# Scaling attention probabilities by products with diagonals on TensorE instead of on GpSimd

## What is computed

```python
def masked_softmax(s, mask):
    s = jnp.where(mask, s.astype(jnp.float32), -jnp.inf)
    m = jnp.max(s, axis=-1, keepdims=True)
    m = jnp.where(jnp.isfinite(m), m, 0.0)
    p = jnp.exp(s - m)
    return p / jnp.maximum(jnp.sum(p, axis=-1, keepdims=True), 1e-30)

s = jnp.einsum('bqhd,bkhd->bhqk', qb, k) * scale
p = masked_softmax(s, pos[None, :] <= t[:, None])
o = jnp.einsum('bhqk,bkhd->bqhd', p.astype(dt), v)
```

## Time and profile before

| | us |
|---|---|
| median of 3 runs | 3665.45 |
| fastest, slowest | 3661.15, 3670.55 |
| the profiled execution | 3661.0 |
| its span | 3659.0 |
| TensorE busy in the span | 3529.5 |

### The profile page before, as it was taken

How to read it: one execution, slowest core, us unless ns; L and a number is a source line. 1 busy time by engine, 2 the same in 40 slices (tenths; PEclk the granted TensorE clock), 3 DMA queues, 4 the chain that set the end, 5 groups by cost and what they waited for, 6 DMA issues and landing times. The chain is left out here.

```text
span 3659.0 us, 46860 instructions
## 1 busy us (share of the span) xinstructions
PE 3529.5 (96%) x16596; PEld 2872.5 (79%) x16596; DVE 2066.9 (56%) x3132; ACT 1399.7 (38%) x2450; POOL 1681.2 (46%) x949
## 2 busy tenths in 40 slices
PE   7999999999999999999999999999999999999998
PEld 5877877788878768778888778778877877778876
DVE  5767646212267767462123676558964665658943
ACT  3244652323233436433322446333333446333332
POOL 3337544444434465444443554434543654435543
PEclk9999999999999999999999999999999999999999
DMA  4310023222232100232243220533343220532322
GB/s 151 109 58 30 28 77 115 86 97 92 98 116 94 52 29 24 89 113 92 92 150 127 76 77 23 184 121 109 126 144 117 70 81 33 177 119 103 132 92 86
DMA packets 96595, 346.73 MB, mean 95 GB/s; under 512 B 12464, under 2 KB 13104, under 8 KB 95792
## 3 DMA queue, kind: packets, MB, share of 16 engines
q1 hardware_dynamic: 96432, 344.61, 27.3%
HBM read 338.14 MB, written 6.29 MB: 94 GB/s over the span
## 5 line engine op out<-in xcount | busy, mean ns | idle before, releaser
L226 POOL TENSOR_TENSOR weights_lo<-arena,weights_hi 128x1024 fp32r<-128x1024 f32 x467 | 1174.9, 2516 | 1516.7 <-ACT weights_hi L200 1515.7
L200 ACT ACTIVATE weights_hi<-arena 128x1024 fp32r<-128x1024 f32 x491 | 517.4, 1054 | 624.8 <-PE ps L608 389.8
L294 PE MATMUL ps<-moving_hi,weights_hi 128*128 128x512 f32 x2448 | 639.0, 400 | 21.7 <-ACT moving_hi L242 9.2
L294 PE MATMUL ps<-moving_hi,weights_lo 128*128 128x512 f32 x2448 | 613.8, 393 | 0.0
L294 PE MATMUL ps<-moving_lo,weights_hi 128*128 128x512 f32 x2448 | 606.0, 389 | 0.3 <-DVE moving_lo L269 0.2
L294 PEld LDWEIGHTS ps<-moving_hi,weights_hi 128*128 128x128 f32 x2448 | 461.2, 189 | 144.3 <-ACT moving_hi L242 13.2
L294 PEld LDWEIGHTS ps<-moving_hi,weights_lo 128*128 128x128 f32 x2448 | 466.4, 191 | 97.6 <-POOL weights_lo L226 0.4
L294 PEld LDWEIGHTS ps<-moving_lo,weights_hi 128*128 128x128 f32 x2448 | 458.4, 188 | 96.3 <-DVE moving_lo L269 0.9
L1043 POOL TENSOR_SCALAR arena<-arena 128x128 f32<-128x128 f32 (+2 forms) x240 | 225.1, 950 | 214.3 <-DVE arena L948 133.4
L247 DVE TENSOR_TENSOR moving_lo<-arena,moving_hi 128x512 fp32r<-128x512 f32 x196 | 177.3, 955 | 233.0 <-ACT moving_hi L242 233.0
L999 ACT ACTIVATE arena<-ps,arena 128x512 f32<-128x512 f32 (+1 forms) x320 | 164.8, 525 | 127.4 <-DVE arena L937 126.5
(11 more groups left out here) (354 smaller groups left out, 5279.4 us busy)
## 6 DMA issues: line engine op xcount, KB each, us to landing
arena<-wstream SPq DMA_DIRECT2D x532, 512.0 KB, 3.3
arena<-modw SPq DMA_DIRECT2D x64, 512.0 KB, 3.6
arena<-modw_first SPq DMA_DIRECT2D x32, 512.0 KB, 4.3
layer_input<-arena SPq DMA_DIRECT2D x2, 2048.0 KB, 6.9
arena<-layer_input SPq DMA_DIRECT2D x2, 2048.0 KB, 8.0
arena<-xT SPq DMA_DIRECT2D x1, 2048.0 KB, 8.7
outT<-arena SPq DMA_DIRECT2D x1, 2048.0 KB, 7.0
arena<-con SPq DMA_DIRECT2D x1, 1411.5 KB, 11.1
```

Source lines behind the costliest of these rows:

```text
L200: m.nc.scalar.activation(m.w_hi[:, j % 2, :], slab(m, base + at), ACT.Copy).then_inc(hi_ready, 1)
L226: m.nc.gpsimd.tensor_tensor(m.w_lo[:, j % 2, :], slab(m, base + (j if at is None else at)), m.w_hi[:, j % 2, :].bitcast(F32), ALU.subtract)\
L294: mm = m.nc.tensor.matmul(bank, unit_tile(w, k), a[:, k, :], start=(p == 0 and k == 0), stop=(p == 2 and k == KD - 1))
```

## The change

VectorE makes four diagonals per unit, one for each query block, in two buffers of four (the tile `spread` is twice as large, which `m.two_tiles` gives). TensorE multiplies all ten blocks by the diagonal of their query block. GpSimd scales nothing, and the semaphore `scaled` is gone. GpSimd still waits for `inverted` before the half of low weights that belongs to a unit.

```diff
-        def diagonal(u):
-            return spread[:, (u % 2) * P:(u % 2 + 1) * P]
+        def diagonal(u, qt):
+            return spread[:, (u % 2 * TT + qt) * P:(u % 2 * TT + qt + 1) * P]
...
             def turn(u):
-                pe.wait_ge(scaled, u + 1)
-                pe.wait_ge(diag_done, u + 1)
+                pe.wait_ge(diag_done, TT * u + TT)
...
-                            if qt < TT - 1:
-                                mm = nc.tensor.transpose(o, block, m.ident)
-                            else:
-                                mm = nc.tensor.matmul(o, block, diagonal(u), start=True, stop=True)
+                            mm = nc.tensor.matmul(o, block, diagonal(u, qt), start=True, stop=True)
...
                 dve.wait_ge(exped, 3 * u + 3)
-                if u >= 2:
-                    dve.wait_ge(scaled, u - 1)
...
-                nc.vector.tensor_scalar(diagonal(u), m.ident, rinv[:, s + 3:s + 4], None, ALU.mult).then_inc(diag_done, 1)
+                for qt in range(TT):
+                    nc.vector.tensor_scalar(diagonal(u, qt), m.ident, rinv[:, s + qt:s + qt + 1], None, ALU.mult).then_inc(diag_done, 1)
...
             for u in range(NU):
-                j, b = divmod(u, nb)
-                s = 4 * (u % 2)
-                pool.wait_ge(inverted, (u + 1) * (1 if weights(j, b) is None else 2))
-                for qt in range(TT - 1):
-                    v = prob[:, u % 2, PROB_AT[qt]:PROB_AT[qt] + P * (qt + 1)]
-                    r = nc.gpsimd.tensor_scalar(v, v, rinv[:, s + qt:s + qt + 1], None, ALU.mult)
-                r.then_inc(scaled, 1)
+                pool.wait_ge(inverted, (u + 1) * (1 if weights(*divmod(u, nb)) is None else 2))
```

More of the change, by code:

```diff
@@ L838, in attention_stage @@
     mx, sums, rinv = m.small[:, 0:8], m.small[:, 8:16], m.small[:, 16:24]
-    with stage(m, "scores maxed exped inverted scaled transposed hi_out lo_out pv_done side_out half_out o_out diag_done tapped "
+    with stage(m, "scores maxed exped inverted transposed hi_out lo_out pv_done side_out half_out o_out diag_done tapped "
                   + Beside.NAMES) as (block, (
-            scores, maxed, exped, inverted, scaled, transposed, hi_out, lo_out, pv_done, side_out, half_out, o_out, diag_done, tapped, *side_sems)):
+            scores, maxed, exped, inverted, transposed, hi_out, lo_out, pv_done, side_out, half_out, o_out, diag_done, tapped, *side_sems)):
         fill = Beside(m, base, gates, 7, side_sems)
@@ L2142, in first_layer @@
     attention_stage(m, 1, lambda j, b: ((m.q_mla[0:MQK, j, :], m.k_mla[0:MQK, j, :]),), lambda j, b, kt: m.r(m.v_mla)[:, kt, j, :],
-                    causal, lambda j, b: None, lambda pair: m.o_mla[:, pair, :], tile(61), gates=gates[3:5], base=C1["gate"] + 3, taps=TAPS_FRONT)
+                    causal, lambda j, b: None, lambda pair: m.o_mla[:, pair, :], m.two_tiles(61), gates=gates[3:5], base=C1["gate"] + 3, taps=TAPS_FRONT)
     compressed_attention_stage(m, gates[5:9], C1["gate"] + 5)
@@ L2149, in first_layer @@
                     lambda j, b, kt: m.r(m.v_nsa)[:, kt, 2 * b + j // 4, :], causal,
-                    lambda j, b: branch[:, :, 3 * j + 1 + b], lambda pair: m.o_nsa[:, pair, :], tile(5), add=True,
+                    lambda j, b: branch[:, :, 3 * j + 1 + b], lambda pair: m.o_nsa[:, pair, :], m.two_tiles(5), add=True,
                     gates=gates[9:14], base=C1["gate"] + 9)
@@ L2712, in second_layer @@
                     lambda j, b, qt: (m.select_bf[qt], 0) if j < NH else (m.causal_bf, qt * P), lambda j, b: None,
-                    lambda pair: (m.o_mla if pair < NH // 2 else m.o_nsa)[:, pair % (NH // 2), :], m.tiles_at(0),
+                    lambda pair: (m.o_mla if pair < NH // 2 else m.o_nsa)[:, pair % (NH // 2), :], m.two_tiles(0),
                     gates=gates[at:at + 5], base=C2["gate"] + at, heads=2 * NH)
@@ L2843, in build @@
         m.v_mla = work(34, 8 * T).rearrange("p (t h d) -> p t h d", t=TT, d=P)
-        m.tiles_at = lambda at: work(at)
+        m.tiles_at, m.two_tiles = lambda at: work(at), lambda at: work(at, 2 * T)
         PADDED = 544
```

## The result

| | before, us | changed, us |
|---|---|---|
| median | 3666.59 | 3725.29 |
| fastest, slowest | 3661.15, 3670.55 | 3723.22, 3727.41 |
| the profiled execution | 3661.0 | 3726.92 |
| its span | 3659.0 | 3725.1 |

The changed kernel is slower by 58.7 us: ratio 1.016, 95% interval 1.0147 to 1.0173. Forecast were 3720 us, with 3707 to 3739, and slower.

A forecast was written before the change was run, and what follows sets the result against it. TensorE was taken to bound the kernel, without room in the attention stages. Profiled 3661.0 + 53.1 (products) + 2 (collision) = 3716.1 us; with the median 4.4 us above that execution, the forecast was 3720 us, range 3707 to 3739.

The forecast's parts named there:

- TensorE is the limit, and the scaling is hidden: Attention stages: TensorE idle only 7.0 of 546.1 us; removing GpSimd's 225.1 us of scaling, all beside TensorE, is worth 0.
- the small room of 0.51 us at the tightest turn: Between the end of GpSimd's scalings and the turn's start: 0.51 us, smallest found in 80 units; others 0.6 to 5.4.
- 53.1 us for the products: TensorE's turn: 20 instructions for 14, at 0.1107 us each; 0.664 us more per unit, 53.1 us over 80 units.
- waits that a longer turn shortens: Copies and subtractions a little less behind after a longer turn, in the few units that wait: 0 to -1 us.
- The added diagonals are covered: VectorE: three more diagonals per unit, 0.59 us, 47 us in all, into 172 us of free time: nothing lost.
- VectorE's idle third: VectorE idle a third of the attention stages, given as an argument against the collision reaching TensorE in full.
- The collision, +2 us: VectorE's diagonals held by GpSimd's low halves in 36 units: 0 to 46 us on VectorE, 0 to 4 reaching TensorE.
- the clock's term: Granted clock in the attention stages: already 1.00, so 0 us; 0.02 x 439 us = 9 us at most returned.
- That the collision reaches TensorE in full: Rival: all 46 us of VectorE's delay by GpSimd's low halves reach TensorE, 3765 us; chance 0.06.
- That part of the 53 us hides: Rival: TensorE's idle time, the clock and modelled matmul ends absorb up to 32 us, down to 3687 us; chance 0.05.
- That the scaling releases the turn: Rival: every turn waits for GpSimd's scaling, so the change gains 102 us, 3563 us; chance 0.02.
- that 20 products fit into the time of 14 instructions: Rival: diagonal products in a run come faster than 0.11 us each, 20 in 1.55 us; 3665 us, chance 0.02.

The follow-up runs named there:

- the products alone: Kernel before with its six transposes per unit made as products with the identity, GpSimd's scaling and single diagonal kept: 3712.05 us, ratio 1.0129.
- moved: Changed kernel with GpSimd making a unit's low half behind VectorE's subtractions of the unit before, not beside the diagonals: 3713.9 us, ratio 1.0137 to the kernel before.
- the kernel with short turns: Changed kernel with the six transposes per unit kept, first three query blocks unscaled: 3705.37 us with low halves beside the diagonals, 3677.9 us with them clear of these.

## Why the prediction was right, point by point

*TensorE is the limit, and the scaling is hidden.* Shown: with the scaling taken away the ratio is 0.9985 to 1.0003 and the stretches differ by 0.2 us, so the small room of 0.51 us at the tightest turn was enough.

*53.1 us for the products.* Shown, with the net 1.9 us too high. In the changed kernel's timeline a turn of a unit of the two-branch attention takes 402.58 - 400.44 = 2.14 us for its 20 instructions:

```profile
400.44 2.39 PE L886 MATMUL ps<-arena 128*128 128x128 f32 x20
402.58 0.70 PE L873 MATMUL ps<-split,split 128*128 128x512 f32 x2
```

The 2.21 us of the forecast were for every turn, read from a latent one; the medians are 2.15, 2.23 and 2.26 us in the three kinds of stage, and 1.47, 1.55 and 1.55 us in the kernel before. The division of a whole turn by 14, 0.1107 us, was a little low for an instruction that is added: it is 0.114. So the turns themselves grew by 54.4 us with the products alone, 1.3 more than forecast. The sum put 0 to -1 us on waits that a longer turn shortens; some 3 us came back that way (TensorE's idle time fell by 2.6 us), and 51.2 us were left.

*The added diagonals are covered.* Right beside the longer turns (0.5 us between the two kernels that differ in them). The reason given was incomplete: they are covered by the longer turn, not by VectorE's idle third. With short turns they cost 13 us.

*The collision, +2 us.* The mechanism was right, the size off by a factor of nearly four: 7.4 us. Its price on VectorE was 32.5 us, within the bounds of 0 and 46. The question whether GpSimd or VectorE would be held was left open. The change shows VectorE held in 32 of 36 cases. The forecast expected the second diagonal to be held, with the first one ahead; that came in 14 cases, and in 18 the first itself was held.
By "SBUF — State Buffer" ("Who interferes with whom") of the Trainium skill the one that issues first keeps the other out for the whole of one instruction. The 14 cases agree with it: the first diagonal ran its 0.29 us and the second waited. In the other 18 the recorded start of the diagonal lies 0.04 us ahead of GpSimd's and still the diagonal waited, so the recorded starts don't tell which of the two issued first.

The term that was mis-sized is the share that reaches TensorE. I counted only the low halves that fall on units with finishing adds, 6 x 0.7 us, and took half of it, without a row that spoke for the half. The trace of the change has three waits of 0.62 to 0.72 us and two of 0.25 us for the subtractions in each two-branch stage, where the kernel before had one of 0.67. Each of the two two-branch stages lost 2.7 us (109.0 against 106.3 and 108.9 against 106.2, changed against moved), together 5.4 of the 7.4 us. The two latent stages together lost 1.7 us, where I had put none. VectorE has the convolution's steps there as well, which may be why; no run tests it.

*Luck.* The two errors point opposite ways, 1.9 us too much for the products and 5.4 too little for the collision. The 55.1 us that the sum forecast and the 58.7 measured are thus nearer to each other than the collision's term deserved. In the clock's term "0.02 x 439" should be 0.02 x 434, which changes nothing in it.

*The clock.* It was 1.00 in the stretches of both kernels; more products and no transposes returned nothing, and lost nothing. "TensorE: Matmul & The Clock Gate" ("Part 4: PE-mode transpose") of the Trainium skill has it that a transpose does not count as activity for the clock gate; with a clock of 1.00 on both sides, these two kernels can't show it. In all four versions that kept short turns and gave TensorE more to wait for, it did fall in some stages: 0.98 and 0.96 for the two-branch attention of the version with all blocks transposed, where TensorE's idle time was 5.8 us of 96. Two of the four have the same six transposes per unit as the kernel before, whose stretches stayed at 1.00 with less idle time, so transposes alone did not lower it. How much of the fall with ten transposes is theirs is open.

*The rivals.* That the collision reaches TensorE in full did not come; on the kernel with short turns, 23 of 32 us did. That part of the 53 us hides was right in kind, with some 3 us and not 32. That the scaling releases the turn is refuted by the kernel without scaling, and that 20 products fit into the time of 14 instructions by the products alone.

## What to carry to other kernels

Where one engine streams without a pause, count its instructions: a multiplication by a diagonal that saves hidden work of other engines was two matmul instructions where a transpose was one, and cost 0.114 us for the one more. Price an addition to a second engine against the room that the same change leaves it: here 36 us of VectorE's side shrank to 8 beside longer turns, and a change that shortened TensorE found VectorE and ScalarE waiting behind and kept 13 of 35 us. When work moves between GpSimd and VectorE, look at what else wakes on the same semaphore; one changed wait took back 7 to 11 us of the loss.

## What the runs showed of the hardware that I had not expected

- A float32 transpose of 128 x 128 and each of the two instructions of a float32 product of that size take the same 0.11 us in a stream by their starts, although the recorded durations of the weight loads differ (142 against 192 ns). Turns with 10, 14, 17 and 20 instructions, in which 10, 6, 3 and 0 of the ten blocks are transposes, take 1.01, 1.47, 1.81 and 2.15 us in the two-branch attention: 0.114 us for each instruction more.
- A run of four VectorE products with a column, each 0.28 us, is not safe from a GpSimd subtraction of 1.27 us that starts within it. One that starts 0.04 us after the first held the first (1.39 us), one that starts 0.10 to 0.21 us after it held the second (1.34 us). Either way the run took 1.9 to 2.0 us.
- GpSimd can be the one that waits. Its first scaling of 128 x 128 took 0.60 us where VectorE made nothing beside it (the version in which GpSimd scales all blocks), 0.69 us behind a diagonal of 0.29 us that had started 0.06 us earlier, and 0.89 us where that VectorE instruction took 0.49 us. VectorE's own was not lengthened in the kernel before (80 times, 285 to 289 ns).
